# Decoder trunk: two projection slabs between the index score units, cached keys multiplied ahead of the prompt attention

## The reference, cut to what matters

```python
def dsa_core(q, qi, wi, qpos, kidx, gather_kv, topk):
    s = jnp.einsum('bthd,bsd->bths', qi, kidx)
    score = jnp.einsum('bths,bth->bts', jax.nn.relu(s), wi)
    score = jnp.where(vis[None], score, -jnp.inf)
    _, idx = lax.top_k(score, topk)
    k_sel, v_sel = gather_kv(idx)
    logits = jnp.einsum('btkgd,btjkd->btkgj', qg, k_sel) * (A_HEAD_DIM ** -0.5)
    logits = jnp.where(valid[:, :, None, None, :], logits, -jnp.inf)
    p = jax.nn.softmax(logits, axis=-1)
    o = jnp.einsum('btkgj,btjkd->btkgd', p, v_sel)
```

## Time and profile before

| | us |
|---|---|
| median of 3 runs | 1835.25 |
| the runs | 1809.63, 1835.25, 1836.64 |
| the profiled execution | 1810.73 |
| its span, first to last instruction | 1808.9 |
| PE busy | 1648.6 (91%) |
| DVE, ACT, POOL busy | 545.2, 536.8, 549.2 (30% each) |

### The profile page before, as it was taken

How to read it: one execution, slowest core, us unless ns; L and a number is a source line. 1 busy time by engine, 2 the same in 40 slices (tenths; PEclk the granted TensorE clock), 3 DMA queues, 4 the chain that set the end, 5 groups by cost and what they waited for, 6 DMA issues and landing times.

```text
span 1808.9 us, 28267 instructions
## 1 busy us (share of the span) xinstructions
PE 1648.6 (91%) x11966; PEld 1525.3 (84%) x11966; DVE 545.2 (30%) x1036; ACT 536.8 (30%) x679; POOL 549.2 (30%) x206
## 2 busy tenths in 40 slices
PE   6887898767889999999988988999998999999996
PEld 5846766544889999999988878778898999999996
DVE  5279835321131101011122676223433111001113
ACT  4342234211233332222234423110333333222231
POOL 5312303111243333334335443000333433333330
PEclk8868957588889999999998998675998999999998
DMA  5313100143112222322222210005322222222221
GB/s 153 113 47 116 46 1 1 37 149 122 66 47 94 93 76 77 104 89 65 73 92 70 65 53 25 1 1 166 125 71 70 73 90 70 93 93 93 67 73 49
DMA packets 116835, 135.98 MB, mean 75 GB/s; under 512 B 5848, under 2 KB 111594, under 8 KB 114705
## 3 DMA queue, kind: packets, MB, share of 16 engines
q1 hardware_dynamic: 112949, 113.91, 20.1%
q0 software_dynamic: 3456, 20.97, 3.3%
q10 hardware_dynamic: 356, 0.03, 0.0%
HBM read 127.14 MB, written 7.94 MB: 75 GB/s over the span
## 4 chain that ended last, share of the span: by engine, by line
PE 81%; DVE 8%; issue 4%; ACT 3%; DMA 2%; POOL 1%; SPq 0%; DVEq 0%; ACTq 0%; POOLq 0%
PE PS L1761 61%; PE PS L1991 2%; PE PS L1961 2%; PE PS L2244 2%; PE PS L2281 2%; PE PS L2242 1%; PE PS L1847 1%; DVE SC L1278 1%; DVE M L1272 1%; PE PS L2056 1%; PE PS L2276 1%; PE PS L2096 1%; PE PS L2260 1%; PE PS L2210 1%; PE PS L1789 1%
## 5 line engine op out<-in xcount | busy, mean ns | idle before, releaser
L1761 PE MATMUL PS<-HHI,WHI 128*128 128x280 f32 x2304 | 646.6, 298 | 21.6 <-DVE HLO L1200 10.8
L1761 PE MATMUL PS<-HLO,WHI 128*128 128x280 f32 x2304 | 641.6, 295 | 0.0
L598 POOL TENSOR_TENSOR WLO<-RAW,WHI 128x2048 fp32r<-128x2048 f32 (+2 forms) x89 | 365.4, 4106 | 781.5 <-ACT WHI L797 591.9
L1761 PE MATMUL PS<-HHI,WLO 128*128 128x280 f32 x2304 | 489.7, 295 | 0.0
L1761 PEld LDWEIGHTS PS<-HHI,WHI 128*128 128x128 f32 x2304 | 443.5, 192 | 26.9 <-issue 17.5
L1761 PEld LDWEIGHTS PS<-HLO,WHI 128*128 128x128 f32 x2304 | 443.0, 192 | 0.0
L1761 PEld LDWEIGHTS PS<-HHI,WLO 128*128 128x128 f32 x2304 | 373.4, 192 | 0.0
L797 ACT ACTIVATE WHI<-RAW 128x2048 fp32r<-128x2048 f32 x87 | 166.1, 1910 | 148.5 <-PE PS L1761 145.9
L1761 PE MATMUL PS<-ALO,WHI 128*128 128x280 f32 x704 | 192.8, 291 | 0.0
L1761 PE MATMUL PS<-AHI,WHI 128*128 128x280 f32 x704 | 192.8, 291 | 0.0
L1536 DVE TENSOR_TENSOR AT<-PS,SG 128x560 f32<-128x560 f32 x44 | 32.6, 742 | 472.7 <-PE PS L1761 472.7
(11 more groups left out here) (300 smaller groups left out, 1747.7 us busy)
## 6 DMA issues: line engine op xcount, KB each, us to landing
RAW<-in_ffn_w_gate SPq DMA_DIRECT2D x22, 1024.0 KB, 5.3
RAW<-in_ffn_w_up SPq DMA_DIRECT2D x22, 1024.0 KB, 5.2
RAW<-in_ffn_w_down SPq DMA_DIRECT2D x16, 768.0 KB, 4.4
RAW<-in_w_in_odd SPq DMA_DIRECT2D x12, 1024.0 KB, 5.3
RAW<-in_ffn_w_down SPq DMA_DIRECT2D x16, 640.0 KB, 4.2
RAW<-in_w_in_even SPq DMA_DIRECT2D x7, 1024.0 KB, 5.2
RAW<-in_w_out_even SPq DMA_DIRECT2D x4, 1024.0 KB, 5.4
SIN<-in_state_gla SPq DMA_DIRECT2D x8, 512.0 KB, 4.1
```

The costliest lines, as they stand in the source:

```text
L598: pool.tensor_tensor(WLO[:, par, 0:kc, :], RAW[:, par, 0:kc, :], WHI[:, par, 0:kc, :].bitcast(F32), ALU.subtract).then_inc(lo_done, 1)
L1761: ins = pe.matmul(acc[a][:, half, 0:HALF], w[:, slot, k, c0:c0 + P], x[:, k0 + k, HALF * half:HALF * half + HALF], start=first and n == 0 ...
```

## The change: what it does

- **Slabs 4 and 5 between the score units.** After each of the 32 score units PE issues one of the 32 inner steps of slabs 4 and 5. ACT's roundings of slabs 5 and 6 and its emptying of `QT` stand between the relus; POOL's remainders of slabs 5, 6 and 7 come earlier. The units' `PS` banks and buffers stay.
- **Cached keys ahead of the prompt attention.** After slabs 6 and 7 (which hold the first 10 `row_total`s) PE runs 32 steps: turn a quarter of a batch's keys into bank 5 or 6, and multiply the quarter before by the queries of that batch into bank c of 0 to 3, in the 32 PSUM rows of the batch. ACT alone empties the turns, into `KTC`, four buffers. 11 further `row_total`s stand after every second step.
- **Logits kept in SBUF.** After batches 0 to 3 and 4 to 7 ACT copies the logits into `SLM`/`SLN`. In the sample attention PE multiplies out the mask alone, and DVE subtracts the logits from it and takes the minimum in one `tensor_tensor_reduce`; ACT's exponential reads SBUF with scale -1.
- **Five buffers for cached rows**: three of `KN`, one in the place of the scratch `NRM`, one in `RAW`'s odd slot. The keys are loaded during stages 3 to 5, values 0 to 3 before POOL's pooling sums, values 4 to 7 in the sample attention. The load of `out0`'s second slab now waits for the values of batch 3 (`spv` 4).
- The weights are turned plain, and the reciprocal is applied when the output rows are copied. The masks of both groups are made first. `QBD` is filled by DVE in round 4 of the search (`queries`), not ahead of the prompt attention. POOL's pooling sums wait for all 32 logits steps (`klog`), since `KTC` shares their place.
- Some semaphores are merged; a few waits of layer 1 count on another semaphore.

The core of the diff:

```diff
@@ PE, score units
                     ins.then_inc(il_ready, 1)
+                    s, j, k = 4 + n // 16, n // 8 % 2, n % 8
+                    if n % 16 == 0:
+                        pe.wait_ge(lo_done, s + 1)
+                    if k == 0:
+                        take(j)
+                    ins = tile_rows(j, s % 2, P * j, [k], 0, HHI, HLO, k == 0, k == KC - 1)
@@ PE, slabs and cached keys
-            for s in range(4, 8):
+            for s in range(6, 8):
...
+            def k_turn(x):
+                b, c = divmod(x, 4)
+                if c == 0:
+                    loaded("k", b)
+                if x >= 2:
+                    pe.wait_ge(turn_ev, x - 1)
+                for j in range(4):
+                    ins = pe.transpose(PS[:, 5 + x % 2, P * j:P * j + P], cached_rows("k", b, 4 * c + j), ident(P))
+                ins.then_inc(turn_tr, 1)
+            def k_logits(x):
+                b, c = divmod(x, 4)
+                rows = slice(32 * (b % 4), 32 * (b % 4) + 32)
+                lhs = QBD[:, b, :, :].rearrange("p k n -> p (k n)")
+                pe.wait_ge(turn_ev, x + 1)
+                if b >= 4:
+                    pe.wait_ge(sl_ev, c + 1 if c < 3 else 5)
+                if c == 3:
+                    pe.matmul(PS[rows, 4, 0:NS], lhs, KT[:, LP:R], start=True, stop=True)
+                pe.matmul(PS[rows, c, :], lhs, KTC[:, x % 4, :], start=True, stop=True).then_inc(klog, 1)
...
+            k_turn(0)
+            for x in range(32):
+                if x + 1 < 32:
+                    k_turn(x + 1)
+                if x % 2 and 10 + x // 2 < SEEK_EARLY:
+                    row_total(10 + x // 2)
+                k_logits(x)
@@ ACT, cached keys
+            for x in range(32):
+                act.wait_ge(turn_tr, x + 1)
+                if x >= 4:
+                    act.wait_ge(klog, x - 3)
+                act.activation(KTC[:, x % 4, :], PS[:, 5 + x % 2, :], ACT.Copy).then_inc(turn_ev, 1)
+                if x in (16, 31):
+                    g = x // 31
+                    for c in range(5):
+                        act.wait_ge(klog, min(16 * g + 13 + c, 16 * g + 16))
+                        if c < 4:
+                            act.activation(SLM[g][:, c, :], PS[:, c, :], ACT.Copy).then_inc(sl_ev, 1)
+                        else:
+                            act.activation(SLN[:, g, :], PS[:, 4, 0:NS], ACT.Copy).then_inc(sl_ev, 1)
@@ DVE, sample attention
+            def sample_max(g):
+                dve.wait_ge(slg_mask, g + 1)
+                dve.tensor_tensor_reduce(SLM[g][:, :, :], SLM[g][:, :, :], PS[:, 0:4, :], -1.0, 3.0e38, ALU.add, ALU.min, STS[:, g, 0:1]).then_inc(smx, 1)
@@ POOL, buffers (name, batch, slot) and releases
+        KV_LOADS = [("k", 0, 3), ("k", 1, 4), ("k", 2, 0), ("k", 3, 1), ("k", 4, 2), ("k", 5, 3), ("k", 6, 4), ("k", 7, 0),
+                    ("v", 0, 1), ("v", 1, 2), ("v", 2, 4), ("v", 3, 0), ("v", 4, 3), ("v", 5, 1), ("v", 6, 2), ("v", 7, 0)]
+                elif kind == "k" and b >= 5:
+                    pool.wait_ge(turn_tr, 4 * (b - 5) + 4)
+                elif kind == "v" and b < 4:
+                    pool.wait_ge(turn_tr, 4 * (3, 4, 6, 7)[b] + 4)
+                elif (kind, b) == ("v", 4):
+                    pool.wait_ge(pv_done, len(UNITS))
+                elif kind == "v":
+                    pool.wait_ge(spv, (1, 2, 4)[b - 5])
@@ PE, sample attention
+            sample_masks(0)
+            sample_masks(1)
+            for g in range(2):
+                sample_flips(g)
+                sample_values(4 * g)
+                sample_values(4 * g + 2)
+                sample_turn(g)
```

More of the change, by code:

```diff
@@ L653, in _ @@
                 kidx(n)
-            for s in range(2, 5):
+            for s in range(2, 6):
                 lo(s)
@@ L676, in _ @@
             pool.affine_select(out=v, in_=v, pattern=[[-1, RB]], compare_op=ALU.is_ge, fill=NEG, base=0, channel_multiplier=1).then_inc(nm_final, 1)
+            for b in range(5, 8):
+                cached("k", b)
+            for b in range(4):
+                cached("v", b)
             pool.wait_ge(acc_free[0], 8)
@@ L716, in _ @@
             lo_at(out0, 0, 0)
-            for q in range(3, 16):
-                cached(q)
+            for b in range(4, 8):
+                cached("v", b)
+            pool.wait_ge(sexp, 2)
             with pool.Fori(0, out0.iters - 1) as i:
@@ L1020, in out_rows @@
+            sample_exp(0)
+            for u in (0, 2, 4):
+                flip_out(0, u)
+            sample_exp(1)
+            sample_hi(0)
+            for u in (0, 2, 4):
+                flip_out(1, u)
+            sample_hi(1)
             def out_rows(name):
@@ L1362, in _ @@
             for r in range(1, ROUNDS_P):
+                if r == 4:
+                    queries()
                 for i in range(1, NRB):
```

399 lines of the change are left out of this document (189 added, 210 removed).

## The result

The changed kernel takes **1830.05 us** (median of 20 executions, 1824.38 to 1840.88); the kernel before takes 1825.36 us beside it (20 executions, 1805.46 to 1836.64). The ratio is 1.0072, 95% interval 1.0048 to 1.0095: within 2%, but slower, where 1799 and a gain were forecast. The profiled execution of the changed kernel took 1830.75 us (span 1829.0, mean granted clock 0.884) against 1810.73 (span 1808.9) before.

A forecast was written before the change was run, and what follows sets the result against it. Taken as bounds: half-clock PE in score units; DVE's rounds, then PE's last slab and POOL's pooling sums; a chain of short steps and loads in the sample attention. +22 + 22 - 68 = -24 from 1823 gave 1799 us, range 1765 to 1836.

The forecast's parts named there:

- Score units, +22: Score units with slab steps between them: 57 us against 35.0, about 10 us at half clock and the rest full.
- bound of +60: Upper bound for the score units: half clock throughout, 2 x 46 + 3 = 95 us.
- Rival (2): Score units stay at half clock because 64-row products dilute the slab steps: +38, execution near 1837; chance 0.08.
- the full case: Score units with slab steps at full clock throughout: 20.6 + 25.6 + 5 for changes, sum 51 us.
- The 0.08 a change: Score units: changing weights and row sets 64 times, some 0.08 us each, 5 us in all.
- The stretch to the prompt attention, +22: From the last score unit to the prompt attention, with 32 key steps at full clock: 133 us against 110.7.
- ACT's five copies: Key steps: at step 16 ACT puts five copies between two turns, of which about 1.7 us show on PE.
- Rival (1): Key steps run at half clock, 2.7 us each: plus 43 us, execution 1830, 1842 at the level used; chance 0.11.
- Prompt attention, 0: The prompt attention's own work, 131.6 us, unchanged: 0, +-4 for where the clock changes fall.
- Sample attention, -68: The sample attention shrinks to 44 us against 111.8; bounds 38 and 56.
- The base: Starting time of the forecast: the mean of four known times of the kernel before, 1823 us.

The follow-up runs named there:

- experiment 3: Changed kernel with two slab steps behind every second score unit in place of one behind each: 1780.0 us, ratio 0.982 to the kernel before.
- experiment 4: Changed kernel with two units then two slab steps, both units of a pair on the same 64 rows: 1791.2 us, ratio 0.983 to the kernel before.
- experiment 6: Changed kernel with four slab steps ahead of the first score unit and none behind the last four: 1785.1 us, ratio 0.983 to the kernel before.
- experiment 7: Changed kernel with five slab steps behind the thirteenth score unit and none behind the last four: 1800.1 us in one execution.
- experiment 5: Changed kernel with score products on 128 rows, plus a 64-row, 8-column product ahead of and behind each unit: 1835.0 us, ratio 1.008 to the kernel before.
- experiment 1: Changed kernel with slabs 4 and 5 back behind the cached index keys: 1790.9 us, ratio 0.986 to the kernel before.
- experiment 8: Changed kernel with slabs 4 and 5 back behind the index keys and score products on 128 rows: 1781.3 us, ratio 0.981 to the kernel before.
- experiment 2: Changed kernel with score products on all 128 rows, zero rows added, same places and columns: 1774.1 us, ratio 0.979 to the kernel before.

## Why the prediction was wrong

- **Score units, +22: the step that failed.** They cost +66.8, past the outer bound of +60. The failing sentence is "I take the value near the full-clock end because the mixture resembles rows 3 more than rows 2". Rival (2), at 0.08, is what happened, but its reason, rows that dilute, is only part of it. The clock had fallen to 0.50 in the pauses ahead of the first unit, six slab products in a row between two changes did not bring it up, and nothing later did. It rose inside runs of 12 together (experiments 3 and 4), of 24 (6) and of 30 (7), and from then on the same mixture ran at 1.00 (in 3 with one fall of 3.3 us). The shares of PE's time were weighed, where the longest dense run had to be.
- **The bound of +60** (2 x 46 + 3 = 95) was short by its pauses. The products alone came out below it: 31 steps of 6 x 0.233 (the last step lies behind the last unit), and 128 score products that start 0.19, 0.28, 0.37 and 0.44 apart by block, make 43 + 41 = 84 us. The changes took the other 17, 0.55 a unit and step, where the full case had 5 and this one 3. The 0.08 a change of the sum was read from no row: a change cost about 0.27 at half clock, and 0.20 at full clock (1.73 a unit and step in experiment 7, of which 1.33 are products).
- **The stretch to the prompt attention, +22: right**, 24.2. First count 46.5 behind the last unit (47.9 forecast), slabs 6 and 7 end at 74.4 (75.5), key steps 51.9 us (48.1) and at 126.2 (123.6), the prompt attention 134.9 (133). A key step was 1.57 and not 1.35, 7 us more in 32 steps; that the sum came out only 4 short is partly luck, since other terms were too large. ACT's five copies, taken at 1.7 us, cost PE nothing: the steps beside them (277.6 to 282.4) are no longer than others. Rival (1), the key steps at half clock, didn't come: PEclk is 1.00 in all 50.0 us from the first turn to the last, and turns by identity are over a third of PE's time there. The Trainium skill ("TensorE: Matmul & The Clock Gate", section Part 4: PE-mode transpose) says that the full clock does not engage for transposes. The traces differ: in the changed kernel the clock came into the key steps at 1.00 and stayed, and in the kernel before it rose from 0.50 to 1.00 at 358.2, within turns alone.
- **Prompt attention, 0: right**, 0.1. Between versions it moved from 126.1 to 132.8 with the places where the clock falls, more than the +-4 allowed.
- **Sample attention, -68: right**, -70.6. The subtract-and-minimum took 2.29 us, for which 2.3 had been taken from the old reduction. Group 1's masks did not run beside it, but began when it had ended (450.37, PE idle 2.62 us before), beside ACT's exponential; they end 10.3 us behind the start, as forecast (10.4).
- **The base.** The mean of the four known times, 1823, was a fair base: the median of 20 is 1825.4. In profiles the forecast was off by 44 us (1787 against 1830.75), in medians by 31, because the profiled execution of before lay low among its times. The failed term alone would have carried 1799 to 1844, past the range's end of 1836. That the result lies inside it is luck: the changed kernel's executions (1824.38 to 1840.88) do not spread upwards from its profile as those of the kernel before do.

With the failed term put right (+67 for +22) the sum is -24 + 45 = +21, and +20.1 was measured.

What stays open: how long a dense run has to be, and why the clock behaves so; the runs show when it rises, not by what rule. Experiment 5 also rose by itself after 72 us, where the products had grown to 224 columns, while the changed kernel, with half as many changes but 64-row products of 224 and 264 columns, did not. So rows and changes both seem to count, and the runs give no measure in which to add them. That rows count by themselves is seen where there is no slab step at all: score units alone stayed at 0.50 on 64 rows and rose to 1.00 after 3.2 us on 128 (experiments 1 and 8).

## What to carry to other kernels

Work set between small products is not free filler on PE: ask first whether the clock falls at the head of the stretch, as it did here within 2 us around the first unit in every run, and whether the first dense run in the new order can raise it. Put a few steps together at its head or put the pieces in pairs; here that moved the same work from 103 us to 51 to 59. And when an interleave is forecast, price the half-clock case from the products' own starts with a pause for each change of row set, and give it a large chance if the units alone never left 0.50.

## What the runs showed of the hardware

- The granted clock depends on what went before: one order of products ran at 0.50 for 101.8 us and, with four steps moved from its end to its head, at 1.00 for 54.7 us; in experiment 7 both are seen within one execution.
- Going from products of 64 rows to products of 128 and back costs pauses: 0.51 to 0.57 us a unit and step for the two changes at half clock (3.67 against 3.16 of products), 0.40 at full clock. With all products on 128 rows they are gone (1.69 against 1.65). 64 products of 8 columns made the units 56 us longer (experiment 5 against 2: 106 against 50).
- Zero rows can pay: the same scores on 128 rows, half of them zero, took 25.8 us in place of 35.2 (experiments 8 and 1), with a mean granted clock of 0.93 in place of 0.52.
- Logits products with 32 columns of weights for two batches, on different columns of the array, take the time of one: 0.98 us for both.
